# A gather ring of six buffers instead of ten, and seven weight half blocks kept on the chip instead of three

## The chip, the cores and the metric

One core of one Trainium2 chip. The metric is the device time of one launch in microseconds (us). The kernel before took 1558.64 us as the median of 3 runs (1556.83 to 1558.65).

## What is computed

A two-layer decoder trunk on 256 tokens of 1024 numbers, in float32. Layer 0 mixes tokens with gated linear attention, layer 1 with differential softmax attention. Each is followed by a PEER channel mixer, which is most of the work: every token looks up 8 heads x 16 experts, fetches one row of `expert_u` and one of `expert_v` for each, and sums them.

```
qry    = (x_blk @ w_query).reshape(T, 8, 2, 128)
scores = einsum('thpd,hpnd->thpn', qry, sub_keys)      # top 16 of 128, twice, then top 16 of 256
u      = expert_u[idx]                                 # T x 8 x 16 rows of 1024
act    = gelu(einsum('thkd,td->thk', u, x_blk))
out    = einsum('thk,thkd->td', gate * act, expert_v[idx])
```

The layer 1 weights that matter here are `diff_w_in` (1024 x 3072), `diff_w_out` (1024 x 1024) and the second `peer_w_query` (1024 x 2048).

## The kernel before, in words

**Pairs.** The 256 tokens are two groups of 128, and each layer treats each group, which gives four tiles of 128 picks: 512 picks (`ROWS`). The u and the v row of an expert lie side by side in memory, so for pick n one indirect DMA of GpSimd (L386) gathers a *pair*, 128 partitions x 2048 floats or 1 MiB, into a buffer. Then VectorE multiplies the u half with the token's row and sums (`dot`, L1525), ScalarE makes gelu, weight and a diagonal matrix (`expert_weight`, L1003, L1006, L1014), and TensorE adds diagonal x v half to the group's sum (`expert_sum`, L608, four passes). The last of these raises `v_used`, which frees the buffer; a few early picks are added on VectorE instead.

**The rings of pair buffers.** `homes()` gives each pick its buffer: for tile 0 from `FIRST` and `EARLY` (ten places), for tiles 1 to 3, picks 128 to 511, from `LATE` (ten places) in turn. GpSimd issues the gathers in order, and each waits for the pick that had the buffer before (L381 to L384). All of it is one in-order queue, so no later gather passes a waiting one.

**Layer 1's weights.** While tiles 1 and 2 are gathered, layer 1 runs once for each token group m (0 and 1): 6 blocks of `diff_in`, 2 of `diff_out`, 4 of `peer_query`. A block is loaded as two *half blocks* of 1 MiB, so 24 for each group, numbered 0 to 23 and 24 to 47: 0 to 11 are `diff_in`, 12 to 15 `diff_out`, 16 to 23 `peer_query`. SyncE issues them in order in `load_halves` (L297 to L317). Most go through a ring of four places (`A_HALF`): a load waits until the half block four earlier in the ring has been used (`half_used`). Those in `KEPT` have a place of their own, are loaded for m = 0 alone, and stay for m = 1 (`if m: continue`). If a kept place is one of `EARLY`, its load waits for the last pick of tile 0 that used it.

**Order of work.** Each engine's order is written out by ticks. In the tick calls `at(t)`, `dot` of pick n stands at tick n + 4 and `expert_sum` at n + 6, and the blocks of layer 1 (`layer1`, `block1`, L636; `query1`, L767; `diff`, L667 to L688) stand between them at times counted in ticks. Layer 1 starts at tick 134 for m = 0 and at 262 for m = 1 (`BASE`). A tick takes as long as the slowest of the engines and the transfers needs for one pick and what stands beside it.

```
KEPT = {4: 24576, 5: 22528, 6: "work3"}
RING = [n for n in range(NT * HALVES) if n % HALVES not in KEPT]
return "kept_loaded", 16 * (len(KEPT) + 1)
at = LATE[(n - SLOTS) % len(LATE)]
sp.wait_ge(S("half_used"), RING[RING.index(n) - 4] + 1)
```

Of the kernel before, what the change touches and what calls it, by code (L numbers as in the profile page):

```python
# [101 lines left out]
A_DV, A_KT, A_KEYT1, A_FINAL = 26624, 28672, 30720, 30720  # L102

HALVES = 24
KEPT = {4: 24576, 5: 22528, 6: "work3"}
RING = [n for n in range(NT * HALVES) if n % HALVES not in KEPT]


def half_at(n):
    return KEPT[n % HALVES] if n % HALVES in KEPT else A_HALF[RING.index(n) % 4]  # L110


def half_loaded(n):
    if n % HALVES in KEPT:
        return "kept_loaded", 16 * (len(KEPT) + 1)
    r = RING.index(n)
    return f"half_loaded{r % 4}", 16 * (r // 4 + 1)
# [2 lines left out]
ROW = 2 * D  # L120
FIRST = ("spare", 8192, 10240, 6144, 24576, 4096)
EARLY = ("spare", 8192, "work0", "work1", 10240, 6144, 24576, 4096, "work2", "work3")
LATE = ("raw0", "raw1", 12288, 14336, 20480, 10240, 6144, 4096, "spare", 8192)


def homes():

    home, turn, before, last, used = [], [], [], {}, {}
    for n in range(ROWS):
# [4 lines left out]
        else:  # L134
            at = LATE[(n - SLOTS) % len(LATE)]
        home.append(at)
# [11 lines left out]
def summed_to(n):  # L148
    return sum(k <= n for k in SUMMED)
# [7 lines left out]
def trunk_kernel(nc, x, x_t, gains_t, positions, norm_ffn, norm_final,  # L157
# [7 lines left out]
    with ctx:  # L165
# [5 lines left out]
        def S(name):  # L171

            if name not in sems:
                sems[name] = ctx.enter_context(nc.semaphore(name))
            return sems[name]
# [96 lines left out]
        def _(sp):  # L272
# [24 lines left out]
            def load_halves(m, first, w, blocks):  # L297

                for j in range(2 * blocks):
                    n = HALVES * m + first + j  # L300
                    if n == 0:
                        sp.wait_ge(S("listed"), NT * LISTS)
                    if n % HALVES in KEPT:
                        if m:
                            continue
                        if KEPT[n] in EARLY:
                            sp.wait_ge(S("v_used"), summed_to(max(p for p in range(SLOTS) if HOME[p] == KEPT[n])))
# [1538 lines left out]
```

## Time and profile before

| | |
|---|---|
| median of 3 runs | 1558.64 us |
| profiled execution, its own time | 1558.8 us |
| its span, first to last instruction | 1557.0 us |
| mean granted TensorE clock | 0.969 |
| PE busy | 1365.5 us, 88% |
| DVE busy | 974.9 us, 63% |
| ACT busy | 673.8 us, 43% |
| POOL busy | 581.7 us, 37% |
| bytes moved | 616.24 MB |
| of these by the gathers' queue (with some early weights) | 551.65 MB |
| by the SyncE queue | 63.31 MB |

PE is TensorE's matmuls, DVE VectorE, ACT ScalarE, POOL GpSimd, SP SyncE. The profile cuts the span in 40 slices and gives the busy share of each in tenths; a 9 is 90% or more. Views by stretch give the busy time of each engine between two times, with the share of the 16 DMA engines that was busy (1.01 is full) and what they moved. A view in order of time gives start, duration, engine, line and tiles of each instruction, and in brackets how long the engine had been idle and what ended that.

### The profile page before, as it was taken

How to read it: one execution, taken by the hardware profiler on the slowest of the kernel's cores; microseconds unless marked ns; L12 is line 12 of the kernel's file. 1: busy time of each engine (PE TensorE's matmuls, PEld its weight loads, DVE VectorE, ACT ScalarE, POOL GpSimd, SP SyncE). 2: the span in 40 equal slices, each digit the busy share in tenths (PEclk: the TensorE clock that was granted, in tenths of full speed). 3: DMA queues.
4: the chain of work that ended last, by engine and by line, in shares of the span. 5: the costliest groups of instructions: out<-in, count | busy, mean ns of one | idle time of the engine just before them, and what ended most of it. 6: DMA issues, size and time to landing. Idle time of an engine off the chain costs nothing.

```text
span 1557.0 us, 15110 instructions
## 1 busy us (share of the span) xinstructions
PE 1365.5 (88%) x4140; PEld 665.8 (43%) x4140; DVE 974.9 (63%) x2429; ACT 673.8 (43%) x1921; POOL 581.7 (37%) x534
## 2 busy tenths in 40 slices
PE   7999998889787998889989799888999978788776
PEld 5554565445322443334555344333565422222222
DVE  5236598988874444664477766565557888554554
ACT  4124443434343244873434434576533434443433
POOL 1002565654442333443333334334444433333331
PEclk9999999999996999999999899999999999999999
DMA  9508999999999999999999999999999999999995
GB/s 383 204 1 363 372 409 425 425 425 425 425 425 422 421 421 422 421 421 421 422 421 421 410 422 421 422 395 402 421 421 420 421 421 422 422 422 421 422 421 236
DMA packets 84946, 616.24 MB, mean 396 GB/s; under 512 B 10336, under 2 KB 10336, under 8 KB 11904
## 3 DMA queue, kind: packets, MB, share of 16 engines
q0 software_dynamic: 75056, 551.65, 85.4%
q1 hardware_dynamic: 9216, 63.31, 9.9%
q8 instruction: 34, 0.56, 0.1%
q10 hardware_dynamic: 592, 0.33, 0.1%
q14 instruction: 48, 0.39, 0.1%
HBM read 614.20 MB, written 1.05 MB: 395 GB/s over the span
## 4 chain that ended last, share of the span: by engine, by line
PE 46%; DMA 34%; ACT 8%; DVE 7%; issue 3%; POOL 1%; ACTq 0%; POOLq 0%; SPq 0%; DVEq 0%
PE banks L608 27%; DMA raw<-in_peer_uv_dram,hnT 13%; DMA arena<-in_peer_uv_dram,hnT 11%; PE banks L636 7%; PE banks L475 5%; DMA work<-in_peer_uv_dram,hnT 5%; DMA spare<-in_peer_uv_dram,hnT 4%; ACT g_e L1014 2%; DVE arena L1525 2%; PE banks L453 2%; PE banks L580 1%; PE banks L767 1%; ACT L1051 1%; ACT hnT L1006 1%; DVE raw L1525 1%
## 5 line engine op out<-in xcount | busy, mean ns | idle before, releaser
L608 PE MATMUL banks<-arena,g_e 128*128 128x512 f32 x1316 | 639.8, 615 | 83.0 <-ACT g_e L1014 81.8
L386 POOL DMA_INDIRECT arena<-in_peer_uv_dram,hnT x332 | 368.9, 1111 | 501.3 <-PE banks L608 467.4
L608 PEld LDWEIGHTS banks<-arena,g_e 128*128 128x128 f32 x1316 | 237.5, 194 | 385.1 <-issue 214.8
L1525 DVE CUSTOM_DVE_ANT_0 arena<-arena,hrows 128x1024 f32<-128x1024 f32 x245 | 298.1, 1222 | 153.4 <-DMA arena<-in_peer_uv_dram,hnT 152.8
L1003 ACT ACTIVATE hnT<-hnT 128x1 f32<-128x1 f32 x512 | 103.3, 202 | 616.5 <-DVE hnT L1525 614.8
L1014 ACT ACTIVATE g_e<-ident,hnT 128x128 f32<-128x128 f32 x500 | 200.8, 402 | 46.7 <-ACT hnT L1006 0.7
L608 PE MATMUL banks<-raw,g_e 128*128 128x512 f32 x312 | 160.2, 640 | 30.8 <-ACT g_e L1014 30.6
L1006 ACT ACTIVATE hnT<-hnT,lists 128x1 f32<-128x1 f32 x512 | 150.7, 294 | 51.8 <-DVE lists L1713 4.2
L1525 DVE CUSTOM_DVE_ANT_0 arena<-arena,banks 128x1024 f32<-128x1024 f32 x89 | 108.5, 1220 | 85.4 <-DMA arena<-in_peer_uv_dram,hnT 83.3
L386 POOL DMA_INDIRECT raw<-in_peer_uv_dram,hnT x78 | 81.3, 1042 | 153.5 <-PE banks L608 152.3
L386 POOL DMA_INDIRECT spare<-in_peer_uv_dram,hnT x52 | 59.0, 1135 | 211.2 <-DVE hnT L1701 105.7
L636 PE MATMUL banks<-arena,work 128*128 128x512 f32 x240 | 116.6, 593 | 1.8 <-ACT work L1036 1.8
L608 PE MATMUL banks<-spare,g_e 128*128 128x512 f32 x196 | 96.4, 615 | 10.8 <-ACT g_e L1014 10.5
L608 PEld LDWEIGHTS banks<-raw,g_e 128*128 128x128 f32 x312 | 57.6, 199 | 110.4 <-ACT g_e L1014 60.5
L608 PE MATMUL banks<-work,g_e 128*128 128x512 f32 x176 | 90.8, 643 | 15.2 <-ACT g_e L1014 15.0
L1525 DVE CUSTOM_DVE_ANT_0 raw<-raw,hrows 128x1024 f32<-128x1024 f32 x52 | 63.5, 1224 | 59.3 <-DMA raw<-in_peer_uv_dram,hnT 59.3
L386 POOL DMA_INDIRECT work<-in_peer_uv_dram,hnT x48 | 62.6, 1305 | 70.4 <-PE banks L608 41.3
L767 PEld LDWEIGHTS banks<-work,arena 128*128 128x128 f32 x512 | 71.8, 196 | 38.8 <-issue 38.8
L1525 DVE CUSTOM_DVE_ANT_0 work<-work,hrows 128x1024 f32<-128x1024 f32 x48 | 58.6, 1221 | 23.7 <-DMA work<-in_peer_uv_dram,hnT 23.5
L767 PE MATMUL banks<-work,arena 128*128 128x128 f32 x512 | 72.2, 279 | 0.0
L636 PEld LDWEIGHTS banks<-arena,work 128*128 128x128 f32 x240 | 45.4, 190 | 59.9 <-issue 56.4
L580 PEld LDWEIGHTS banks<-arena 128*128 128x128 f32 x384 | 53.3, 194 | 29.2 <-issue 29.2
(263 smaller groups left out, 1293.4 us busy)
## 6 DMA issues: line engine op xcount, KB each, us to landing
arena<-in_diff_in_dram SPq DMA_DIRECT2D x20, 1024.0 KB, 9.8
arena<-in_peer_query_dram SPq DMA_DIRECT2D x16, 1024.0 KB, 9.5
arena<-in_gla_in_dram POOLq DMA_DIRECT2D x5, 2048.0 KB, 19.8
arena<-in_diff_out_dram SPq DMA_DIRECT2D x8, 1024.0 KB, 9.1
arena<-in_peer_query_dram SPq DMA_DIRECT2D x3, 2048.0 KB, 11.8
arena<-in_peer_uv_dram,hnT POOLq DMA_INDIRECT x336, 19.7
work<-in_gla_out_dram POOLq DMA_DIRECT2D x2, 2048.0 KB, 39.4
arena<-in_gla_in_dram SPq DMA_DIRECT2D x2, 1024.0 KB, 12.7
```

The lines of the kernel that those rows point to most:

```text
L386: pool.indirect_dma_start(pair(n), None, table, bass.IndirectOffsetOnAxis(ap=places[:, o:o + 1].bitcast(u32), axis=0)).then_inc(S(f"pair_l ...
L453: last = nc.tensor.matmul(dst[:, j * SEQ:(j + 1) * SEQ].rearrange("p (m t) -> p m t", m=NT), w, hnT[:, :, k, :], start=(k == 0), stop=(k = ...
L475: last = nc.tensor.matmul(dst, hnT[:, m, k, :], w[:, k * 512:(k + 1) * 512], start=(k == 0), stop=(k == KD - 1))
L580: last = nc.tensor.matmul(dst[:, g * P:(g + 1) * P], query_block(b)[:, k * 512 + g * P:k * 512 + (g + 1) * P], ar(A_HN + m * D + k * P, P) ...
L608: last = nc.tensor.matmul(bank(2 * (tile % NT) + half), diags[:, slot * P:(slot + 1) * P], v_row(n)[:, half * 512:(half + 1) * 512], start ...
L636: last = nc.tensor.matmul(dst, x1(X_T, k * P, P), half_block(halves, k % (KD // 2)), start=(k == 0), stop=(k == KD - 1))
L767: last = nc.tensor.matmul(bank(4 + b)[:, g * P:(g + 1) * P], w, x1(X_T, k * P, P), start=(k == 0), stop=(k == KD - 1))
L1003: A(dots[:, o:o + 1], dots[:, o:o + 1], ACT.Gelu).then_inc(S("gelu_done"), 1)
L1006: A(weights[:, o:o + 1], dots[:, o:o + 1], ACT.Copy, scale=ls(L_GG + o, 1)).then_inc(S("weighted"), 1)
L1014: A(diags[:, turn % DIAGS * P:(turn % DIAGS + 1) * P], ident[:], ACT.Copy, scale=weights[:, o:o + 1]).then_inc(S("diag_ready"), 1)
L1051: last = A(x1(X_P, n % 2 * 512 + half * 256, w), x1(X_S, n % 2 * 512 + half * 256, w), ACT.Exp, bias=stat[:, 52 + (n % 2) * 2 + half:53 + ...
L1525: V.tensor_tensor_reduce(out=u_row(n), in0=u_row(n), in1=normed, scale=1.0, scalar=0.0, op0=ALU.mult, op1=ALU.add, accum_out=dots[:, o:o + ...
```

## The change

Two tables are edited, nothing else.

```diff
-KEPT = {4: 24576, 5: 22528, 6: "work3"}
+KEPT = {4: 24576, 5: 22528, 6: "work3", 7: 8192, 8: 4096, 9: 6144, 10: 10240}
...
-LATE = ("raw0", "raw1", 12288, 14336, 20480, 10240, 6144, 4096, "spare", 8192)
+LATE = ("raw0", "raw1", 12288, 14336, 20480, "spare")
```

Four places of the second pair ring become homes of the half blocks 7 to 10 of `diff_in`. They are loaded for m = 0 and not again for m = 1. The count that the first use of any kept half block waits for becomes 16 x 8.

SP, the queue of weight loads, at the half blocks 6 to 23 of m = 0 and 0 to 23 of m = 1 (before with -, the change with +; diff_in, diff_out and peer_query are the weights, arena the place they go to):

```order
 L313 DMA work<-in_diff_in_dram 128x1024 [waits v_used]
 L313 DMA hnT<-in_diff_in_dram 128x1024
-L316 DMA arena<-in_diff_in_dram 128x2048 [waits half_used] x5
+L316 DMA arena<-in_diff_in_dram 128x2048 [waits v_used] x4
+L316 DMA arena<-in_diff_in_dram 128x2048 [waits half_used]
 L316 DMA arena<-in_diff_out_dram 128x2048 [waits half_used] x4
 L316 DMA arena<-in_peer_query_dram 128x2048 [waits half_used] x8
-L316 DMA arena<-in_diff_in_dram 128x2048 [waits half_used] x9
+L316 DMA arena<-in_diff_in_dram 128x2048 [waits half_used] x5
```

Half blocks 7 to 10 now wait for picks of tile 0 instead of used half blocks, so they stand directly behind 0 to 6, and 11 to 14 take the turns in the ring that 7 to 10 had; of m = 1's nine loads of `diff_in` five are left.

POOL, the queue of gathers, at the start of the second ring, before (raw, arena and spare are the buffers):

```order
L386 DMA raw<-in_peer_uv_dram,hnT 128x2048 [waits scores_done,listed]
L386 DMA raw<-in_peer_uv_dram,hnT 128x2048
L386 DMA arena<-in_peer_uv_dram,hnT 128x2048 x3
L386 DMA arena<-in_peer_uv_dram,hnT 128x2048 [waits v_used] x3
L386 DMA spare<-in_peer_uv_dram,hnT 128x2048 [waits v_used]
L386 DMA arena<-in_peer_uv_dram,hnT 128x2048 [waits v_used]
```

and with the change:

```order
L386 DMA raw<-in_peer_uv_dram,hnT 128x2048 [waits scores_done,listed]
L386 DMA raw<-in_peer_uv_dram,hnT 128x2048
L386 DMA arena<-in_peer_uv_dram,hnT 128x2048 x3
L386 DMA spare<-in_peer_uv_dram,hnT 128x2048 [waits v_used]
L386 DMA raw<-in_peer_uv_dram,hnT 128x2048 [waits v_used] x2
L386 DMA arena<-in_peer_uv_dram,hnT 128x2048 [waits v_used] x3
```

The raw buffers come again after six gathers instead of ten, so each gather waits for the sum of the pick six before it instead of ten before it.

## Rows read from the trace of the kernel before

**Rows 1.** The page: DMA busy in tenths and GB/s, 40 slices of the span.

```profile
DMA  9508999999999999999999999999999999999995
GB/s 383 204 1 363 372 409 425 425 425 425 425 425 422 421 421 422 421 421 421 422 421 421 410 422 421 422 395 402 421 421 420 421 421 422 422 422 421 422 421 236
```

**Rows 2.** By stretch: length, PE, PEld, DVE, ACT, POOL busy (count), clock, DMA share, GB/s.

```profile
500.00:605.00 105.00, 105.00 (x258) 47.01 (x257) 45.67 (x85) 40.27 (x122) 40.51 (x35) 1.00 1.01 421
605.00:620.00 15.00, 9.15 (x26) 3.42 (x25) 7.36 (x15) 7.43 (x20) 5.16 (x5) 1.00 1.02 423
690.00:735.00 45.00, 43.40 (x117) 20.43 (x116) 20.84 (x39) 19.25 (x58) 15.49 (x15) 0.98 1.01 421
890.00:987.00 97.00, 97.00 (x242) 43.68 (x241) 63.15 (x166) 35.85 (x107) 37.74 (x33) 1.00 1.01 420
987.00:1112.00 125.00, 107.19 (x306) 49.09 (x304) 75.03 (x163) 81.46 (x219) 50.91 (x44) 0.97 1.00 407
1112.00:1155.00 43.00, 42.21 (x183) 25.89 (x184) 23.41 (x50) 20.28 (x59) 19.56 (x18) 1.00 1.01 422
1182.00:1540.00 358.00, 293.30 (x696) 116.09 (x697) 224.18 (x501) 145.09 (x447) 136.20 (x138) 0.98 1.01 419
```

**Rows 3.** In order of time, SP's weight loads: start, length of the run, loads.

```profile
452.88 6.09 SPq L316 DMA_DIRECT2D arena<-in_diff_in_dram  x6
510.62 55.26 SPq L316 DMA_DIRECT2D arena<-in_diff_in_dram  x5
822.19 121.91 SPq L316 DMA_DIRECT2D arena<-in_diff_in_dram  x9
954.95 24.36 SPq L316 DMA_DIRECT2D arena<-in_diff_out_dram  x4
```

**Rows 4.** In order of time, DVE and POOL around 546 to 552.

```profile
546.61 1.23 DVE L1525 CUSTOM_DVE_ANT_0 raw<-raw,hrows 128x1024 f32<-128x1024 f32 x1 [1.26 <-DMA raw<-in_peer_uv_dram,hnT]
...
552.06 1.55 POOL L386 DMA_INDIRECT raw<-in_peer_uv_dram,hnT  x1 [0.93 <-PE banks L608]
```

**Rows 5.** In order of time, DVE and POOL around 1414 to 1419.

```profile
1414.01 1.22 DVE L1525 CUSTOM_DVE_ANT_0 raw<-raw,banks 128x1024 f32<-128x1024 f32 x1 [1.26 <-DMA raw<-in_peer_uv_dram,hnT]
...
1416.49 1.22 DVE L1525 CUSTOM_DVE_ANT_0 raw<-raw,banks 128x1024 f32<-128x1024 f32 x1 [1.25 <-DMA raw<-in_peer_uv_dram,hnT]
...
1418.66 0.94 POOL L386 DMA_INDIRECT raw<-in_peer_uv_dram,hnT  x1 [1.54 <-PE banks L608]
```

**Rows 6.** DMA issues with us to landing: at 119.9, at 181, at 184.9, and 1040 to 1062.

```profile
spare<-in_peer_uv_dram,hnT POOLq DMA_INDIRECT x1, 5.8
...
work<-in_peer_uv_dram,hnT POOLq DMA_INDIRECT x1, 7.6
...
work<-in_peer_uv_dram,hnT POOLq DMA_INDIRECT x1, 8.0
...
arena<-in_peer_uv_dram,hnT POOLq DMA_INDIRECT x6, 11.8
```

**Rows 7.** Waits of the stretch 980 to 1000: us in total, times, longest.

```profile
DVE spare L1525 <- DMA spare<-in_peer_uv_dram,hnT: 3.7, 1, 3.7
DVE raw L1525 <- DMA raw<-in_peer_uv_dram,hnT: 3.0, 2, 1.7
...
DVE arena L1525 <- DMA arena<-in_peer_uv_dram,hnT: 1.9, 1, 1.9
```

**Rows 8.** In order of time, DVE and POOL around 1125 to 1134.

```profile
1125.65 1.23 DVE L1525 CUSTOM_DVE_ANT_0 raw<-raw,hrows 128x1024 f32<-128x1024 f32 x1 [1.25 <-DMA raw<-in_peer_uv_dram,hnT]
...
1133.90 1.28 POOL L386 DMA_INDIRECT raw<-in_peer_uv_dram,hnT  x1 [1.26 <-PE banks L608]
```

**Rows 9.** In order of time, two late issues of POOL, and the DVE row before one.

```profile
1221.27 1.21 DVE L1525 CUSTOM_DVE_ANT_0 arena<-arena,hrows 128x1024 f32<-128x1024 f32 x1
...
1230.42 0.94 POOL L386 DMA_INDIRECT arena<-in_peer_uv_dram,hnT  x1 [4.89 <-PE banks L608]
...
1344.90 0.94 POOL L386 DMA_INDIRECT raw<-in_peer_uv_dram,hnT  x1 [2.01 <-PE banks L608]
1353.42 0.94 POOL L386 DMA_INDIRECT arena<-in_peer_uv_dram,hnT  x1 [7.59 <-PE banks L608]
```

## The prediction

> **What bounds the kernel now.** I read the page first, for the engine that has no gaps. The DMA row is at 9 in all slices but a few at the start and one at each end, and the rate lies near 421 GB/s [rows 1]. So the transfers are the nearest thing to a bound, and four loads of 1 MiB fewer look like a plain gain. Then I read the same time by stretch, because a share of the whole span mixes stages with different limits. There the picture divides [rows 2]. In 500:605 and in 890:987, where the input blocks of layer 1 are multiplied for the two token groups, PE is busy for all of the time: 105.00 of 105.00 and 97.00 of 97.00 us. DMA is full there as well, but it does not have to be: it fills the ring ahead of PE. In 1182:1540 it is the other way round, PE 293 of 358 us and DMA full, so there the transfers set the pace.
>
> The time of one pick under that pace is read from two dots in a row, 1414.01 and 1416.49, both of which waited for their transfer: 2.48 us for each MiB [rows 5]. The same group gives how long a buffer is held. The raw buffer whose dot begins at 1414.01, as it lands, is gathered into again at 1418.66: 4.65 us for dot, weight, sum and the wake-up of POOL. The third number is the lead, from the issue of a gather to its landing. It is long when ten are queued and says nothing then. Where few were queued it is 5.8 for the very first, 7.6 and 8.0 for two with the engines already at work, and 11.8 as the median of a stretch with some queue in front [rows 6]. I take 8.0, the larger of the two that had a running engine and hardly a queue, with 5.8 and 10.2 as ends (10.2 is what six buffers leave, below).
>
> So one turn of a buffer needs 4.65 + 8.0 = 12.65 us. Ten buffers at 2.48 us give it 24.8, six give 14.9. Six therefore carry the steady pace with 2.25 us to spare, where ten had 12.15. Whatever holds a buffer longer than that now stops the transfers.
>
> **The change part by part.**
>
> *The four loads that go.* In m = 1 half blocks 7 to 10 are not loaded again: 4 x 2.48 = 9.9 us of DMA time. They lie among the nine loads that begin at 822.19 and run on to 944 [rows 3], so all but the first few in 890:987. PE has not one idle microsecond there, and its work stays as it is, so that stretch cannot become shorter. What the saved transfers could do instead is run ahead with pairs, but the ring that would hold them is the one that is cut. They are worth only the waits right behind: in 980 to 1000 DVE waits 3.7 + 3.0 + 1.9 us for pairs [rows 7]. The 3.7 lies under PE's full stretch; of the other 4.9 I take 2, because what follows in 987:1112 is a chain in which DMA is at 407 GB/s, below its pace [rows 2], so pairs are soon ready too early. Term C: -2, with ends at -8.6 and 0.
>
> *The same loads in m = 0, moved forward.* Half blocks 7 to 10 used to be issued between 510.62 and about 535 as ring places came free [rows 3]. Now they stand behind 0 to 6, wait for the last picks of tile 0 alone, and follow the six that were issued at 452.88; 11 to 14 take over the ring turns from 510 on. So by about 545 the engines have moved four half blocks more than before, and four pairs fewer: 9.9 us. Before, the sum at that place came just in time: the pair that lands at 546.61 has its buffer back at 552.06, 5.45 us, only 0.8 over the least hold [rows 4, 5]. So PE, which was full, gets 9.9 - 0.8 = 9.1 us of gaps. Later the DMA engines have less to load and PE no longer waits: of 605:620 it stood idle for 15.00 - 9.15 = 5.85 us [rows 2], and that goes. Term A: 9.1 - 5.85 = +3. Ends: -6, if the gaps do not come, and +9, if nothing is given back.
>
> *Six buffers, first group's output blocks, 690:735.* PE is at 43.40 of 45 [rows 2], and 15 gathers are issued, so a pick takes 3.0 us and six picks 18, more than 12.65. A little is lost because four loads of query weights come in the same time. Term B: +1, ends 0 and +4.
>
> *Six buffers, second group, 987:1155.* In 1112:1155 a buffer is held for 8.25 us, from the dot at 1125.65 to the next gather at 1133.90 [rows 8], though DMA is full there: pairs land 8.25 - 4.65 = 3.6 us earlier than needed. That store was built in 987:1112, where the pairs waited longer still, and it is used up by the query loads behind it. With six buffers, 8.25 + 8.0 = 16.25 is over 14.9, so it cannot be built, and the pace behind 1155 is DMA's. Term D: +3.6, ends 0 and +9.9 (all four buffers at 2.48).
>
> *Six buffers, single late buffers in the tail.* The pair whose dot starts at 1221.27 gives its buffer back at 1230.42, after 9.15 us; 9.15 + 8.0 - 14.9 = 2.25 us. At 1344.90 POOL issues, and then not until 1353.42, because DVE makes the first group's final rows: 8.52 - 2.48 = 6.04 us late, less the 2.25 to spare, 3.8 us [rows 9]. With ten buffers both were covered. The tail is at DMA's pace, so such a gap is not caught up. Term E: 2.25 + 3.8 = +6. With a lead of 5.8 the two give about +1; with 10.2 nothing is to spare, and they cost 4.5 + 6.0 = 10.5.
>
> The Trainium skill speaks against this lead. "DMA: Bandwidth & Descriptors", section "Anatomy of one DMA — SWDGE (gpsimd) path", gives a fixed 2.0 us and bytes at 436 GB/s, which I estimate as 4.4 us for 1 MiB. The shortest of the rows is 5.8, so the row decides. By the page's figure term E would be nothing and the sum 6 us less.
>
> ACT's order stays the same, and the dots, sums and weights are as many as before, with the same lengths, in other buffers. That costs nothing in itself. The first use of a kept half block now waits for all seven; the last of them should land about 20 us before block 2 needs it, so that wait costs nothing, and if they landed late it would be part of term A.
>
> Sum: A 3 + B 1 + C -2 + D 3.6 + E 6 = +11.6 us. The sum is against the profiled execution, 1558.8 us (span 1557.0), which is 0.2 us above the median of the runs. Forecast: **1570 us**.
>
> **The rivals.**
>
> *The bytes pay in full, faster.* DMA is at 1.01 of its time in nearly every stretch, so 9.9 us less work would end 9.9 us earlier: 1549. This needs that no stretch makes DMA wait for a buffer, and that PE's full stretches still have slack inside their busy time. For it: the steady turn of 12.65 us fits into 14.9. Against it: PE at 97.00 of 97.00 where the loads go, and holds of 8.25 and 9.15 us. It decides from a lead below about 5.8 us together with a PE that can run faster in 890:987. Chance 0.12. [...]
>
> *Six buffers are enough, but the saved loads lie under PE.* Then A, B, D and E are near nothing and C alone is left: 1557, between 1554 and 1561. It needs a lead of about 6 us, which one row has. Chance 0.17, of which 0.03 is faster by more than the bound below.
>
> *Six buffers do not even carry the steady pace.* With the 11.8 us of 1040 to 1062 as the lead, a turn needs 4.65 + 11.8 = 16.45, or 2.74 us for each pick. The 138 gathers of 1182:1540 [rows 2] would cost 0.26 us each, 36 us, with the rest about 1606. Against it: part of that 11.8 is queue, and a shorter ring has a shorter queue. Chance 0.08.
>
> That the change does not do what it says I leave out: the listing of SP's queue has four loads fewer.
>
> **How the numbers follow.** My own case has 0.63; its range by the ends of its terms is 1562 to 1586, with E from 1 to 10.5 and A to 9 as the widest. A difference of 0.2%, about 3.1 us, is what a measurement of this kernel can tell from none. Faster: 0.12 + 0.03 = 0.15. Within: 0.14. Slower: 0.63 + 0.08 = 0.71. The range of 8 in 10 takes in the second rival and my own case, 1555 to 1586; below it lies the first rival, above it the third.
>
> **What the profile of the changed kernel would show.** SyncE's queue moves 4.2 MB less. If I am right, the DMA share falls below 1.00 in the second group's input blocks and in 987:1112, while PE stays full through those input blocks and they last 97 us as before; the dots between about 515 and 555 come some 9 us later than before; and gaps of DMA follow the two late buffers of the tail. Time from issue to landing falls from about 20 to about 10 us in the tail. Wrong would be: a DMA share at 1.01 throughout with an earlier end (first rival), input blocks of the second group that become shorter, or a tail in which two dots in a row are 2.7 us apart (third rival).

## The result and the profile after

The changed kernel takes **1581.77 us**, the median of three runs (1581.74 to 1584.39), the kernel before 1558.64. A fourth run was a slow one of 4817.66 us; with it the median is 1583.08, and it stands in no comparison here. The ratio is 1.0153 with a 95% interval of 1.0139 to 1.0167: slower by 23.8 us (21.7 to 26.0). The forecast was 1570, so the direction was right and the size less than half. The profiled execution took 1581.77 us, its span is 1580.0 (before 1557.0).

The page of the changed kernel, DMA busy in tenths and GB/s over 40 slices, and the SyncE queue:

```profile
DMA  9409999999999999999999999999999999999997
GB/s 384 194 1 372 363 411 424 425 425 425 425 424 422 421 379 384 386 374 406 421 421 421 370 422 390 389 337 389 416 421 421 404 423 421 396 417 421 422 421 307
...
q1 hardware_dynamic: 8640, 59.12, 9.1%
```

The queue moved 59.12 MB instead of 63.31, so the four loads are gone. The digits of the DMA row say nothing: 9 is "90% or more". The row below it does. Of the slices near 421 in [rows 1], the 15th to the 18th, from the first group's input blocks to its output blocks, are at 374 to 386 now. Of the 23rd to the 28th, from the stretch ahead of the second group's input blocks to its attention, all but one are at 337 to 390. In the tail it is near 421 again but for the 32nd and the 35th, 404 and 396, where the two late buffers of [rows 9] lie.

The same by stretch, for stretches that hold about the same work as those of the kernel before, moved where the changed kernel is later, by up to 23 us (columns as in [rows 2]; the fourth belongs to 1040:1112, which is shown in experiment 1, the others to rows of [rows 2]):

```profile
500.00:605.00 105.00, 96.14 (x229) 41.24 (x228) 45.10 (x84) 38.53 (x119) 33.12 (x33) 1.00 1.00 398
...
700.00:750.00 50.00, 47.16 (x128) 22.54 (x126) 22.29 (x40) 20.04 (x61) 17.01 (x16) 0.95 0.99 396
...
904.00:1001.00 97.00, 96.97 (x241) 43.34 (x240) 64.12 (x167) 36.30 (x107) 35.91 (x33) 1.00 1.00 401
...
1051.00:1133.00 82.00, 70.45 (x182) 32.28 (x181) 41.80 (x88) 44.09 (x127) 27.23 (x27) 0.93 0.95 375
...
1205.00:1563.00 358.00, 290.61 (x695) 114.32 (x694) 223.44 (x501) 144.48 (x445) 136.34 (x142) 0.99 1.01 416
```

The first row has PE 105.00 - 96.14 = 8.9 us short of full, where the forecast had gaps of 9.1. The second group's input blocks are the third row: 97 us as before, PE full, DMA with 401 instead of 420 GB/s. Fewer bytes are moved there, and that shortens nothing there. (The share of busy DMA time is 1.00 there, not below 1.00 as the prediction had it among its signs; only the rate shows the change.) The fourth row, the second group's attention, is the worst: 375 GB/s. The fifth, the tail, is nearly what it was.

SyncE's weight loads in order of time, answering [rows 3]:

```profile
454.35 6.12 SPq L316 DMA_DIRECT2D arena<-in_diff_in_dram  x6
...
482.60 33.51 SPq L316 DMA_DIRECT2D arena<-in_diff_in_dram  x5
...
835.10 67.37 SPq L316 DMA_DIRECT2D arena<-in_diff_in_dram  x5
```

Half blocks 7 to 11 are issued from 482.60 on, 28 us earlier than before, and five loads stand where nine stood.

How late the changed kernel is along the run is read from the last matmul of the same pick's sum in both traces, in us:

| pick | 128 | 164 | 172 | 196 | 216 | 260 | 304 | 336 | 360 | 384 | 440 | 508 |
|---|---|---|---|---|---|---|---|---|---|---|---|---|
| the change | 1.1 | 11.7 | 5.8 | 9.6 | 15.0 | 13.3 | 11.4 | 16.9 | 22.9 | 21.9 | 23.7 | 23.7 |

The table counts from the first instruction of each trace. Four places lose: the input blocks of the first group (to pick 164, half of it given back by 172), its attention and output blocks (172 to 216), and the second group's attention (304 to 336) and output and query blocks (336 to 360). One wins, behind the second group's input blocks (260 to 304). The tail adds less than 2 us.

### The profile page after: what moved, and what is told of

The parts are those of the page before. It is cut to its first block, busy times and chain, and to the rows that moved or that the text cites. A ratio compares the mean times of both kernels' runs of the same rounds, so it can differ in the third digit from the quotient of the medians.

```text
span 1580.0 us, 15106 instructions
## 1 busy us (share of the span) xinstructions
PE 1367.2 (87%) x4140; PEld 663.9 (42%) x4140; DVE 977.1 (62%) x2429; ACT 674.9 (43%) x1921; POOL 565.2 (36%) x534
## 3 DMA queue, kind: packets, MB, share of 16 engines
q1 hardware_dynamic: 8640, 59.12, 9.1%
## 4 chain that ended last, share of the span: by engine, by line
PE 46%; DMA 33%; ACT 9%; DVE 7%; issue 4%; POOL 1%; ACTq 0%; SPq 0%; DVEq 0%; POOLq 0%
PE banks L608 29%; DMA arena<-in_peer_uv_dram,hnT 15%; DMA raw<-in_peer_uv_dram,hnT 6%; DMA work<-in_peer_uv_dram,hnT 6%; PE banks L636 5%; DMA spare<-in_peer_uv_dram,hnT 5%; PE banks L475 4%; ACT g_e L1014 3%; DVE arena L1525 2%; PE banks L453 2%; PE banks L767 2%; PE banks L580 1%; ACT hnT L1006 1%; ACT L1051 1%; ACT hnT L1003 1%
## 5 line engine op out<-in xcount | busy, mean ns | idle before, releaser
L608 PE MATMUL banks<-arena,g_e 128*128 128x512 f32 x1012 | 503.0, 625 | 88.4 <-ACT g_e L1014 87.7
L386 POOL DMA_INDIRECT arena<-in_peer_uv_dram,hnT x257 | 278.4, 1083 | 433.3 <-PE banks L608 404.5
L1525 DVE CUSTOM_DVE_ANT_0 arena<-arena,hrows 128x1024 f32<-128x1024 f32 x194 | 237.0, 1224 | 154.2 <-DMA arena<-in_peer_uv_dram,hnT 153.7
L608 PEld LDWEIGHTS banks<-arena,g_e 128*128 128x128 f32 x1012 | 183.5, 196 | 328.2 <-ACT g_e L1014 169.1
L608 PE MATMUL banks<-raw,g_e 128*128 128x512 f32 x512 | 246.0, 607 | 34.2 <-ACT g_e L1014 33.8
L386 POOL DMA_INDIRECT raw<-in_peer_uv_dram,hnT x128 | 134.0, 1047 | 211.2 <-PE banks L608 210.0
L608 PE MATMUL banks<-spare,g_e 128*128 128x512 f32 x300 | 150.0, 624 | 22.7 <-ACT g_e L1014 22.7
L1525 DVE CUSTOM_DVE_ANT_0 spare<-spare,hrows 128x1024 f32<-128x1024 f32 x56 | 68.4, 1222 | 47.1 <-DMA spare<-in_peer_uv_dram,hnT 47.0
L608 PEld LDWEIGHTS banks<-spare,g_e 128*128 128x128 f32 x300 | 55.1, 197 | 93.5 <-issue 49.6
L1525 DVE CUSTOM_DVE_ANT_0 raw<-raw,banks 128x1024 f32<-128x1024 f32 x42 | 51.2, 1220 | 43.3 <-DMA raw<-in_peer_uv_dram,hnT 43.3
## 6 DMA issues: line engine op xcount, KB each, us to landing
arena<-in_peer_query_dram SPq DMA_DIRECT2D x3, 2048.0 KB, 11.9
arena<-in_peer_uv_dram,hnT POOLq DMA_INDIRECT x259, 10.2
```

Source lines behind the costliest of these rows:

```text
L386: pool.indirect_dma_start(pair(n), None, table, bass.IndirectOffsetOnAxis(ap=places[:, o:o + 1].bitcast(u32), axis=0)).then_inc(S(f"pair_l ...
L608: last = nc.tensor.matmul(bank(2 * (tile % NT) + half), diags[:, slot * P:(slot + 1) * P], v_row(n)[:, half * 512:(half + 1) * 512], start ...
L1525: V.tensor_tensor_reduce(out=u_row(n), in0=u_row(n), in1=normed, scale=1.0, scalar=0.0, op0=ALU.mult, op1=ALU.add, accum_out=dots[:, o:o + ...
```

## The experiments

**Theory 1**, formed from the table: six buffers are too few beside layer 1's attention and output blocks, and the transfers stop there. **Rival 2**: the loads moved forward carry most of the loss. **Rival 3**: the four saved loads pay in full, and an even larger cost of the ring hides it. Theory 4, formed later, is theory 1 as a rule: a stage loses where hold plus lead is over ring size x pace.

All ratios are against runs of the kernel before on the same chip. Microseconds from a ratio are (ratio - 1) x 1558.6.

**1. The parts of the change, one by one.** The ring of six alone; the four loads left out alone, with ten buffers; the change without the early loads:

```diff
ring6_kept3 (from the kernel before)
-LATE = ("raw0", "raw1", 12288, 14336, 20480, 10240, 6144, 4096, "spare", 8192)
+LATE = ("raw0", "raw1", 12288, 14336, 20480, "spare")
ring10_skip4 (from the kernel before)
+SAME = {n: 4 + n % 2 for n in range(HALVES + 7, HALVES + 11)}
 def half_at(n):
+    n = SAME.get(n, n)
...
+                    if n in SAME:
+                        continue
kept7_late (from the changed kernel)
+OWN = (7, 8, 9, 10)
+TURN = sorted(RING + list(OWN))
...
+                        if n in OWN:
+                            sp.wait_ge(S("half_used"), TURN[TURN.index(n) - 4] + 1)
```

> The ring cut to six alone; kept half blocks stay three, so all 24 MiB of layer 1's weights of the second group but three are loaded again and nothing is loaded earlier. Theory 1, six buffers are too few wherever sums of pairs stand behind layer 1's attention and output blocks: the shifts read from the two traces there, 3.8 + 5.4 us for the first group, 11.5 for the second, 1.8 in the tail, make +22, so about 1581 us. Rival 2, the ring costs what the prediction's terms B, D and E say (+10.6) and the rest of the loss is that of the loads moved forward: about 1569 us. Rival 3, the saved loads do pay in full and only a larger cost of the ring hides it: about 1583 + 10 = 1593 us.

> The kernel before with ten buffers, but the second group does not load half blocks 7 to 10; their multiplications read the kept half blocks 4 and 5 in their place (so this part of layer 1's input projection is computed with other weights). It measures what 4 MiB less is worth by itself. Theory 1: the shift read behind the second group's input blocks is -2.2 to -3.6 us, so 1555 to 1556.5 us. Rival 3, the bytes pay in full: 4 x 2.48 = 9.9 us, about 1549 us. A third answer, no gain at all as PE has no gap there: 1558.6 us.

> The change, but half blocks 7 to 10 of the first group are loaded into their kept places at the time that the kernel before loads them (each waits until the half block four earlier in the order of loads has been used, and 11 to 14 wait for 7 to 10), with a semaphore of their own. It takes term A away. Theory 1: the gaps of PE between 515 and 555 us go, which cost 10 us there, and so does what was given back until 620; the net is the 4.3 us that the traces show at that point, so about 1579 us. Rival 2, the loads moved forward carry most of the loss: 1572 us or less. If the 4.3 us are covered later by a stretch that waits for something else, 1583 us as the change.

| | median us | ratio, 95% interval | us |
|---|---|---|---|
| ring6_kept3 | 1585.49 | 1.0171 [1.0157, 1.0185] | +26.7 |
| ring10_skip4 | 1552.01 | 0.9959 [0.9945, 0.9972] | -6.4 |
| kept7_late | 1578.17 | 1.0126 [1.0111, 1.0142] | +19.6 |

The ring alone costs more than the whole change. Theory 1 was 4.7 us short, and rivals 2 and 3 are out as they were put: rival 2 had the ring at 10.6 us, rival 3 at some 34. The four loads are worth 6.4 us with ten buffers, more than theory 1's 2.2 to 3.6 and less than the 9.9 of their bytes; with six they are worth 26.7 - 19.6 = 7.1. Loading them early costs 23.8 - 19.6 = 4.2 us, an estimate, as the two intervals overlap a little. The parts add up: 26.7 - 6.4 + 4.2 = 24.5, against 23.8 measured. As the 4.2 is itself taken from the 23.8, what this checks is 26.7 - 6.4 = 20.3 against the 19.6 of kept7_late.

Where the ring of six alone loses is seen by stretch. The ring of six, and then the kernel before:

```profile
620.00:690.00 70.00, 54.33 (x152) 23.16 (x152) 45.45 (x108) 56.65 (x153) 26.95 (x27) 1.00 1.00 402
690.00:735.00 45.00, 44.03 (x113) 21.11 (x114) 19.56 (x35) 15.58 (x53) 13.93 (x13) 0.93 0.97 383
...
860.00:890.00 30.00, 20.53 (x48) 9.31 (x48) 21.66 (x66) 13.84 (x40) 8.55 (x8) 0.83 0.87 354
...
987.00:1040.00 53.00, 43.07 (x117) 18.56 (x116) 33.32 (x71) 35.43 (x87) 17.27 (x17) 0.90 0.96 385
1040.00:1112.00 72.00, 61.52 (x162) 27.86 (x161) 41.74 (x89) 44.86 (x131) 26.36 (x24) 0.95 0.98 376
1112.00:1155.00 43.00, 39.67 (x136) 21.58 (x136) 19.94 (x35) 19.81 (x51) 15.64 (x15) 0.92 0.98 402
```

```profile
620.00:690.00 70.00, 57.61 (x155) 24.77 (x156) 47.15 (x113) 56.32 (x154) 27.59 (x26) 0.96 1.01 421
...
860.00:890.00 30.00, 20.82 (x44) 9.15 (x45) 22.76 (x72) 13.96 (x40) 9.11 (x7) 0.77 1.00 410
...
987.00:1040.00 53.00, 41.79 (x124) 18.89 (x123) 36.34 (x79) 39.31 (x96) 20.26 (x18) 0.94 1.01 417
1040.00:1112.00 72.00, 65.41 (x183) 30.20 (x181) 38.69 (x85) 42.15 (x124) 30.65 (x26) 1.00 0.99 399
```

Read the last column as time: (421 - 402)/421 x 70 = 3.2 us of transfers not made in the first row, then, with [rows 2] for the second and the sixth, 4.1, 4.1, 4.1, 4.2 and 2.0. That is 21.7 of the 26.7 us, spread over six stretches. These were picked; the whole of layer 1 says the same, the ring of six first, then the kernel before:

```profile
480.00:1180.00 700.00, 620.65 (x1820) 301.22 (x1819) 398.26 (x931) 334.19 (x941) 252.97 (x229) 0.96 0.99 403
```

```profile
480.00:1180.00 700.00, 635.48 (x1920) 312.54 (x1919) 412.05 (x984) 340.86 (x967) 265.06 (x239) 0.96 1.01 418
```

(418 - 403)/418 x 700 = 25.1 us. So nearly all of the loss is time in which the transfers did not run. Why they did not is seen from the gathers that are under way, from issue to landing. In this stretch the kernel before always has four or more. The ring of six is 30.7 us' worth of transfers short of 421 GB/s, and 28.4 of them fall where three gathers or fewer are under way. One such stop, POOL and then the stretch in it, with DMA at 3 GB/s:

```profile
877.62 0.94 POOL L386 DMA_INDIRECT arena<-in_peer_uv_dram,hnT  x1 [5.69 <-PE banks L608]
887.19 1.39 POOL L386 DMA_INDIRECT spare<-in_peer_uv_dram,hnT  x1 [8.64 <-PE banks L608]
```

```profile
886.00:889.00 3.00, 3.00 (x7) 1.27 (x6) 3.00 (x12) 2.27 (x9) 1.39 (x1) 0.75 0.01 3
```

POOL waits for PE's sum to give a buffer back, and the transfers run dry.

In kept7_late the first row of the profile after is whole again:

```profile
500.00:605.00 105.00, 103.52 (x251) 45.95 (x252) 45.00 (x84) 39.84 (x121) 38.46 (x35) 1.00 1.00 409
```

PE is at 103.52 against 96.14, so most of the gaps did come from the early loads. (The profiled execution of kept7_late took 1573.69 us, 4.5 less than the median of its runs.) In ring10_skip4 the waits of VectorE of [rows 7] are gone altogether; all that is left of its waits in 980 to 1000 is not for pairs:

```profile
DVE work L1435 <- PE banks L672: 9.0, 1, 9.0
DVE stat L1449 <- ACT work L1056: 4.8, 2, 2.4
```

**2. Six buffers in one tile of 128 picks at a time**, ten in the others (a pick takes the allowed buffer that was used longest ago):

```diff
+FEW = ("raw0", "raw1", 12288, 14336, 20480, "spare")
+FEW_AT = range(138, 256)
...
+            if n >= SLOTS + len(LATE):
+                at = min(FEW if n in FEW_AT else LATE, key=lambda p: last[p])
```

> Three kept half blocks; the ring has six buffers for picks 138 to 255 only (the first group's layer 1) and ten elsewhere. The ring of six alone, in its own trace, is 7.1 us late at pick 256, nearly all of it gained at picks 196 to 216, beside the first group's output blocks. If that loss stays, as the engines have no slack behind it: +7, about 1566 us. The prediction's term B: +1, 1560 us. If ten buffers win it back in the second group: under 1561 us.

> Three kept half blocks; six buffers for picks 256 to 383 only (the second group's layer 1). In the trace of the ring of six alone the shift grows there from 7.1 to 23.3 us (input blocks +4, attention +4, output and query blocks +8): +16, about 1575 us. The prediction's term D: +3.6, 1562.5 us.

> Three kept half blocks; six buffers for picks 384 to 511 only (the tail behind layer 1). In the trace of the ring of six alone the shift grows there from 23.3 to 26.3 us: +2 to +3, about 1561.5 us. The prediction's term E (lead 8.0 us): +6, 1565 us; with its steady pace missed: more. If six are enough in the tail: 1559 us.

| | median us | ratio, 95% interval | us |
|---|---|---|---|
| six_tile1, first group | 1563.43 | 1.0033 [1.0021, 1.0045] | +5.1 |
| six_tile2, second group | 1574.81 | 1.0111 [1.0095, 1.0126] | +17.3 |
| six_tile3, tail | 1558.60 | 1.0005 [0.9996, 1.0014] | +0.8 |

They sum to 23.2 of 26.7. The second group carries two thirds, and the tail, where the forecast had put its largest term, nothing that can be told from zero (-0.6 to 2.2 us). In the tail of six_tile3 the second late buffer of [rows 9] comes again (in order of time, POOL's gathers at L390 and VectorE's dots):

```profile
1343.77 0.94 POOL L390 DMA_INDIRECT arena<-in_peer_uv_dram,hnT  x1 [2.06 <-PE banks L612]
...
1352.25 0.94 POOL L390 DMA_INDIRECT arena<-in_peer_uv_dram,hnT  x1 [7.55 <-PE banks L612]
...
1355.61 1.22 DVE L1529 CUSTOM_DVE_ANT_0 arena<-arena,banks 128x1024 f32<-128x1024 f32 x1 [1.37 <-DMA arena<-in_peer_uv_dram,hnT]
...
1358.09 1.22 DVE L1529 CUSTOM_DVE_ANT_0 arena<-arena,banks 128x1024 f32<-128x1024 f32 x1 [1.25 <-DMA arena<-in_peer_uv_dram,hnT]
...
1360.56 1.22 DVE L1529 CUSTOM_DVE_ANT_0 arena<-arena,banks 128x1024 f32<-128x1024 f32 x1 [1.24 <-DMA arena<-in_peer_uv_dram,hnT]
...
1364.43 1.22 DVE L1529 CUSTOM_DVE_ANT_0 spare<-spare,banks 128x1024 f32<-128x1024 f32 x1 [2.64 <-DMA spare<-in_peer_uv_dram,hnT]
```

the transfers issued at 1352.25 and at 1354.90, with us to landing, and the stretch ahead of them:

```profile
arena<-in_peer_uv_dram,hnT POOLq DMA_INDIRECT x1, 5.8
...
arena<-in_peer_uv_dram,hnT POOLq DMA_INDIRECT x1, 5.6
```

```profile
1351.50:1353.50 2.00, 2.00 (x4) 0.70 (x3) 0.49 (x1) 0.32 (x1) 0.94 (x1) 0.50 0.15 61
```

POOL stops for 8.48 us, as in the kernel before (8.52). But by then DMA has nearly run dry (a share of 0.15 and 61 GB/s), and the gather issued at 1352.25 lands after 5.8 us, in time for the dot at 1358.09, 2.48 us after the one before. The next has that one ahead of it and lands after 5.6. The dot that comes late is that at 1364.43, by 3.87 - 2.48 = 1.4 us; the one behind it adds 0.3.

**3. Is it the store of landed pairs that the query loads use up?** The second group's eight query half blocks are not loaded, with ten and with six buffers (the same edit as ring10_skip4, for half blocks 40 to 47).

> Ten buffers, three kept half blocks, but the second group does not load its eight half blocks of query weights; their multiplications read the kept half blocks 4 and 5 (that part is computed with other weights). Beside the run with six buffers it tells what the store of landed pairs is for. The eight loads are 8 x 2.48 = 19.8 us of DMA time; PE's own work of that stretch (42.21 of 43 us busy) lets little of it be won: between 1545 and 1555 us.

> The same with six buffers. Theory 1, the store: pairs that land ahead beside the second group's attention are spent while DMA carries the query weights, and six buffers cannot hold them. Without these loads nothing is spent there, so of the 26.6 us that six buffers cost with the loads the 8 to 12 us of the second group's attention and query blocks go, and six cost 15 to 19 us over ten buffers without the loads. Rival, the long holds themselves stop the engines wherever they come, whatever else is loaded: still 24 to 27 us over ten buffers without the loads. If all of the loss behind the first group hangs on these loads: 9 us or less.

| | median us | ratio, 95% interval | us |
|---|---|---|---|
| ring10_noquery | 1542.39 | 0.9896 [0.9879, 0.9912] | -16.2 |
| ring6_noquery | 1574.10 | 1.0096 [1.0079, 1.0113] | +15.0 |

Six buffers cost 16.2 + 15.0 = 31.2 us without these loads, more than the 26.7 with them. So the theory of the store fell, at least as the whole of it. Ten buffers turn 16.2 of the 19.8 us into time; six only 26.7 - 15.0 = 11.7. In the stretch where the loads were, ten and then six buffers:

```profile
1112.00:1155.00 43.00, 41.95 (x179) 25.06 (x178) 24.71 (x54) 20.82 (x61) 20.74 (x18) 1.00 1.00 406
```

```profile
1112.00:1155.00 43.00, 40.66 (x146) 22.09 (x145) 20.55 (x38) 20.88 (x54) 16.82 (x16) 1.00 0.97 377
```

With six, the same loads are left out and DMA moves less than with ten. That it waits for buffers there too is argued from experiment 1; these two rows do not show it.

**4. Is it the time for which a buffer is held?** The sums of picks 160 to 370 stand one tick earlier, with ten and with six buffers:

```diff
-SUM_T = [n + LANDED + SUM_LAG for n in range(ROWS)]
+SUM_T = [n + LANDED + (SUM_LAG if n < 160 or n > 370 else 1) for n in range(ROWS)]
```

> Ten buffers; the sum of each pick 160 to 370 stands one tick earlier in PE's order (one tick behind its dot instead of two), so a buffer is given back up to 2.5 to 3 us earlier. A control for the next run: with ten buffers the holds are covered, so at best nothing, 1558.5 us; or slower by some us, where PE now waits for the diagonal of a pick whose weight is not made yet.

> Six buffers and three kept half blocks, with the sums of picks 160 to 370 one tick earlier. Theory 1: what counts is the time for which a buffer is held, and 2.5 to 3 us less is what one more buffer gives; eight buffers in place of six won back 23.5 us, about 12 for each, so about 1573 us against 1585.5. Rival, the loss is the number of pairs that can lie ready, whatever the order of the sums: 1583 to 1587 us. If PE then waits for the diagonals in its order, as much slower as the kernel with ten buffers is by this edit.

ring10_lag1 took 1559.03 us, ratio 1.0007 [0.9998, 1.0017]: no change that can be told. ring6_lag1 took 1578.81, ratio 1.0128 [1.0111, 1.0145], against 1.0171 [1.0157, 1.0185] of the ring of six alone: 6.7 us won by earlier sums, where ten buffers win none. The size is about half of what theory 1 expected, and shorter holds are seen only in part: from the trace of the ring of six to that of ring6_lag1 the mean time from dot to sum falls from 8.5 to 7.6 us for picks 196 to 215, and stays for 262 to 299 (6.9 and 6.9) and for 320 to 339 (8.0 and 8.0). So this run speaks for the holds without showing that they are all of it.

**5. How the loss falls with the size of the ring** (8192 and 4096 left out of `LATE` for eight, 6144 too for seven; three kept half blocks).

> A ring of eight (arena places 8192 and 4096 left out), three kept half blocks. A turn of eight buffers at 2.48 us is 19.8 us. Theory 1: beside the second group's attention a buffer is held 12 to 17 us with ten buffers and the lead is 6 to 8 us, 18 to 25 together, so eight lose a little there: +2 to +8, 1561 to 1567 us, much less than six. The prediction's own reckoning, that a turn needs 12.65 us and only single holds exceed it: no loss, 1558 to 1560 us. If the loss grows evenly with each buffer taken away: half of that of six, about +11, 1570 us.

> A ring of seven, three kept half blocks. Theory 4, a stage loses when hold from landing to sum (without the wait for the dot) plus lead is over ring size x pace: beside the output blocks and the second group's attention that is 9 to 10 + 8 to 9 = 17 to 19 us; six buffers give 16.7 to 18.2 at 2.79 to 3.03 us per pick, seven give 19.5 to 21.2. So seven are just enough on the mean and lose only where single holds are longer: +4 to +8, 1562 to 1566 us, near the ring of eight (+2.8). Rival, the loss falls evenly from six (+26.6) to eight (+2.8): +14.7, 1573 us.

| buffers | 6 | 7 | 8 | 10 |
|---|---|---|---|---|
| median us | 1585.49 | 1567.96 | 1561.99 | 1558.64 |
| ratio, 95% interval | 1.0171 [1.0157, 1.0185] | 1.0052 [1.0036, 1.0067] | 1.0018 [1.0009, 1.0027] | 1 |
| us | +26.7 | +8.1 | +2.8 | 0 |

The loss does not fall evenly: the step from seven to six costs 18.6 us, that from eight to seven 5.3. Seven gave 8.1 us, at the upper end of the 4 to 8 that were expected by theory 4, and far from the 14.7 of an even fall.

**6. Versions between.** The change with both repairs; eight buffers and five kept half blocks (7 and 8, loaded late), without and with earlier sums of picks 312 to 352; nine buffers and four kept half blocks (7, loaded late).

> The change with half blocks 7 to 10 loaded late and with the sums of picks 160 to 370 one tick earlier: both repairs together. If they add up, each as measured alone (-5 and -6.7): 1583 - 11.7 = 1571.5 us. If the saved loads already cover what the earlier sums win: 1575 to 1578 us. In neither case below the kernel before, as six buffers still hold too little beside the second group's attention.

> A middle way: eight buffers and five kept half blocks (7 and 8 beside 4, 5, 6), these two loaded when the kernel before loads them. If the parts add up: ring of eight +3.0 and half of the 6.9 us that four loads less gave: -3.4, so about 1558.5 us, no difference that can be told. If the saved loads pay only where the ring is short too, as 4 to 5 us for four loads: 1559.5 us. Faster than 1555 would mean that the ring's loss and the saved loads lie at the same place and cancel there.

> Eight buffers, five kept half blocks, 7 and 8 loaded late, and the sums of picks 312 to 352 one tick earlier, where the run without that lost 3.7 us that it had won before. If shorter holds win that back: 1554 to 1555.5 us, below the kernel before. If PE then waits for diagonals as with ten buffers (+1): 1557 to 1558 us.

> Nine buffers, four kept half blocks, half block 7 loaded late. By the rule nine lose nothing (9 x 2.79 = 25.1 us against 17 to 25), and one load less is worth a quarter of 6.4 us: 1557 us. If nine lose as much as one load gives: 1558.5 us.

| | median us | ratio, 95% interval | us |
|---|---|---|---|
| kept7_late_lag1 | 1576.12 | 1.0100 [1.0084, 1.0115] | +15.6 |
| kept5_ring8_late | 1557.40 | 0.9994 [0.9985, 1.0003] | -0.9 |
| kept5_ring8_lag1 | 1559.59 | 1.0004 [0.9995, 1.0013] | +0.6 |
| kept4_ring9_late | 1556.65 | 0.9987 [0.9978, 0.9996] | -2.0 |

The two repairs together win 8.2 us of the change's 23.8, not the 10.9 that they sum to. Eight buffers give back what two saved loads win, and earlier sums do not help there, a miss. Nine buffers with one load saved are 2.0 us below the kernel before. The interval does not hold 1, but the gain is under the 0.2% that the prediction took as its bound. It is the fastest version here that loads all of its weights.

## Why the prediction was wrong

Its terms beside what the runs give for each:

| term | forecast us | measured us | by |
|---|---|---|---|
| A, early loads in m = 0 | +3 | +4.2 | the change less kept7_late |
| B, first group | +1 | +5.1 | six_tile1 |
| C, saved loads | -2 | -6.4 | ring10_skip4 |
| D, second group | +3.6 | +17.3 | six_tile2 |
| E, tail | +6 | +0.8 | six_tile3 |

The 0.8 of E cannot be told from nothing, and the 4.2 of A is the difference of two intervals that overlap.

**Right.** A in size and, in the trace of the changed kernel, in both of its halves: 9.1 us of gaps forecast, 8.9 found in 500:605, and 11.7 - 5.8 = 5.9 us given back by pick 172, forecast 5.85. Some of this is luck: kept7_late, in which nearly all of the gaps are gone, is also 4.1 us later at pick 172 than at pick 128, the change 4.7. PE stays full through the second group's input blocks, and they last 97 us. The bytes do not pay in full. The steady pace is carried by six: two dots of the tail of the changed kernel are 2.47 us apart,

```profile
1417.84 1.22 DVE L1525 CUSTOM_DVE_ANT_0 arena<-arena,banks 128x1024 f32<-128x1024 f32 x1 [1.25 <-DMA arena<-in_peer_uv_dram,hnT]
1420.31 1.22 DVE L1525 CUSTOM_DVE_ANT_0 spare<-spare,banks 128x1024 f32<-128x1024 f32 x1 [1.24 <-DMA spare<-in_peer_uv_dram,hnT]
```

against 2.48 in [rows 5], and the time from issue to landing fell from 20.2 to 10.2 us, as forecast. So all three rivals are out.

**Wrong, B and D: the hold.** The step that failed is "15 gathers are issued, so a pick takes 3.0 us and six picks 18, more than 12.65". The 12.65 holds 4.65 us for dot, weight, sum and wake-up, read in the tail, where nothing stands between them. Beside layer 1 the sum waits in PE's order behind the blocks. Two places of the trace of the kernel before show how long. A raw buffer beside the first group's output blocks, and the spare one beside the second group's attention, each with its dot and its next gather:

```profile
713.01 1.22 DVE L1525 CUSTOM_DVE_ANT_0 raw<-raw,hrows 128x1024 f32<-128x1024 f32 x1
...
724.94 0.94 POOL L386 DMA_INDIRECT raw<-in_peer_uv_dram,hnT  x1 [2.49 <-PE banks L608]
```

```profile
1092.29 1.22 DVE L1525 CUSTOM_DVE_ANT_0 spare<-spare,hrows 128x1024 f32<-128x1024 f32 x1
...
1104.22 0.94 POOL L386 DMA_INDIRECT spare<-in_peer_uv_dram,hnT  x1 [2.50 <-PE banks L608]
```

From dot to next gather they take 11.9 us both, not 4.65. For D the prediction read one hold, 8.25 us at 1125 [rows 8], where it was already short again, and the step that failed is "so it cannot be built": it charged the lost store once, 3.6 us, and not a stop at each place where a buffer comes back too late. With the ring of six the same is seen as a turn, for one raw buffer, from gather to dot to next gather (rows of raw that are left out belong to the other raw buffer):

```profile
1088.68 0.94 POOL L386 DMA_INDIRECT raw<-in_peer_uv_dram,hnT  x1 [1.57 <-PE banks L608]
...
1096.33 1.22 DVE L1525 CUSTOM_DVE_ANT_0 raw<-raw,hrows 128x1024 f32<-128x1024 f32 x1 [1.22 <-DMA raw<-in_peer_uv_dram,hnT]
...
1106.67 1.83 POOL L386 DMA_INDIRECT raw<-in_peer_uv_dram,hnT  x1 [1.64 <-PE banks L608]
```

7.65 us to the dot and 10.34 us on to the next gather make 17.99, so six buffers give one pick in 3.0 us here, where the kernel before has a pace of 2.79. The table puts theory 4 by stage, from the means over the picks of a stage (issue, landing, dot and last matmul of the sum of each, in the traces of the kernel before and of the ring of six; the pace is from dot to dot); the last column is how much later the sums of the ring of six are at the end of the stage than at its start:

| picks | dot to sum, before | lead with six | together | six x pace of before | lost with six |
|---|---|---|---|---|---|
| 196 to 215, first output blocks | 8.9 | 9.5 | 18.4 | 18.2 (3.03) | 6.2 |
| 262 to 299, second input blocks | 10.7 | 11.4 | 22.1 | 18.0 (3.00) | 4.1 |
| 320 to 339, second attention | 9.9 | 9.2 | 19.1 | 16.7 (2.79) | 8.0 |
| 384 to 507, tail | 4.7 | 10.1 | 14.8 | 15.1 (2.51) | 3.0 |

The rule names the stages, and the tail as the one that has what it needs (3.0 us were lost there in this trace, 0.8 in the runs of six_tile3), but it sizes only one of them. In the third stage six buffers are short by 2.4 us, or 0.4 for each pick, and the pace measured there with six is 3.18, 0.39 more. In the first it gives 0.2 us for six picks, under 1 us for the stage, and 6.2 were lost. In the second it gives 4.1 us for each six of 38 picks, some 26, and 4.1 were lost in all. There the hold itself gave way: with six the mean from dot to sum is 6.9 us, as a pair that comes later waits less for the same sum. In the third it fell too, to 8.0, so that 0.39 meets 0.4 is in part luck. Nor does the loss grow with each pick: in the trace of the ring of six the sums are 4.0 us late at pick 200 and still at 210, 7.5 at 216, 11.5 at 320, 16.4 at 325, 15.3 at 335 and 19.5 at 340. It comes in single stops, such as the one at 877.62 in experiment 1; which hold makes each of them was not followed.

The second line was in no term: the forecast had the input blocks of the second group as PE's, and overlooked that ten buffers are filled in the 30 us before them (410 GB/s in 860 to 890, with six 354, the stop at 877.62 among them). In the trace of the ring of six it costs 11.2 - 7.1 = 4.1 us, the shifts at picks 304 and 260. That gathers which wait for a buffer stop the transfers is shown by experiment 1, and that this happens beside layer 1 and hardly in the tail by experiment 2. That it is the length of the holds is supported by the earlier sums (experiment 4) and fits the steep step from seven buffers to six (experiment 5), and the rival that the query loads spend a store of landed pairs does not explain it (experiment 3). A turn of means is not the whole: at seven it would foresee nothing in the third stage, and 8.1 us were lost in all.

**Wrong, E: the lead.** The step is "I take 8.0, the larger of the two that had a running engine and hardly a queue". Each of these two, at 181 and 184.9 in [rows 6], had two other gathers still under way: of those ahead of the first, one is issued at 173.47 and lands 10.2 us later, one at 177.62 and lands 8.5 us later. After the stop of POOL a gather lands 5.8 us after its issue, and the four gathers in all these traces that were issued with no other under way took 5.9 to 6.2. The prediction had said that with 5.8 the two late buffers give about +1 (its own terms make it 0.05 + 1.6); 0.8 was measured, between -0.6 and 2.2. The Trainium skill's "DMA: Bandwidth & Descriptors", section "Anatomy of one DMA — SWDGE (gpsimd) path", by which I had estimated 4.4 us for 1 MiB, was nearer to these rows than the 8.0: less the 0.94 us of POOL's own instruction the 5.8 is 4.9.

**Wrong, C: the size.** The step is "of the other 4.9 I take 2, because what follows in 987:1112 is a chain". The pair waits went altogether. In the trace of ring10_skip4 the sums are 1.2 us early ahead of the skipped loads (pick 260), 4.6 behind them (pick 304) and 7.0 at the end. So 3.4 us come there, and 2.4 more later, between picks 340 and 384, beside the query loads. So pairs that are ready early seem to pay once the transfers are late again, which the term had denied; no run tests this by itself. The Trainium skill's "Perfetto Trace Analysis", section "Identifying the Most-Contended Engine", has the most contended engine optimized first, and for DMA goes by HBM utilization, the bytes moved against what the memory can give, in place of occupancy. With ten buffers fewer bytes did pay, 6.4 of 9.9 us; but the buffers given for them, which kept DMA busy, cost 26.7.

B and D together are 17.8 us too small, A 1.2. C and E are 4.4 and 5.2 us too high, which hid half of that error in the sum. That the forecast came as near as 12 us is luck to that extent.

## What to carry to other kernels

A ring of buffers has to be sized for each stage of the program: the hold in that stage, from landing to the last reader's end, plus the shortest lead, against the number of buffers times the pace. Read the hold in the stage where the most other work stands between first and last reader, not where the rows are cleanest. This tells which stages to fear and not what they will lose: here it gave under 1 us where 6.2 were lost, and 26 where 4.1 were, because holds shorten when pairs come later and single stops do not show in a mean. And where transfers set the end, compare the moved bytes by stretch and not the busy share: in 1040:1112, 98% busy against 99% hid 376 GB/s against 399.

## What the runs showed of the hardware that was not expected

The time from issue to landing of a 1 MiB gather followed the queue closely: 20.2 us with ten buffers in the tail, 10.2 with six, and 5.9 to 6.2 with no other gather under way. A ring cut to six pulled its own lead down, and in the tail of six_tile3 a gap of 8.5 us in the issues became one of 1.4 us at the dots. And the share of busy DMA time overstates the rate: in the ring of six it stood at 0.97 and 0.98 in stretches with 383, 376 and 402 GB/s, 5 to 11% under 421.
